# Layer 1 attention of a hybrid decoder trunk: order of VectorE's masks and denominators, place of the routing steps, engine of the softmax divisions

## The reference, cut to what matters

```python
q, k, v = split(rmsnorm(h) @ w_qkv + b_qkv)          # 16 query heads, 2 key heads, 64 wide; then partial rotary
scores = einsum(q_block, [previous_block, this_block] keys) * 64 ** -0.5   # blocks of 128 tokens
m = max(max(where(valid, scores, -inf)), sink);  p = exp(scores - m)
denom = sum(p) + exp(sink - m)
o = (p @ v) / denom
h = h + o @ w_o + b_o
u = rmsnorm(h)                                       # router: best of 4 groups, then the 2 best of its 8 experts
h = h + mixture_of_experts(u)                        # exact dispatch: each token's place in its expert's block is needed
```

## Time and profile before

| what | value |
|---|---|
| median of 3 executions | 2166.18 us (2165.95 to 2168.13) |
| profiled execution, its own time | 2168.93 us |
| span of the profiled execution | 2167.2 us |
| mean granted TensorE clock | 0.976 of full |
| busy: TensorE, VectorE, ScalarE, GpSimd | 2057.6, 1618.5, 1369.8, 240.6 us |

### The profile page before, as it was taken

One profiled execution on the slowest core, in us unless ns is written; L12 is line 12 of the kernel. 1 busy time (PEld: TensorE's weight loads), 2 busy tenths in 40 slices (PEclk: granted clock), 3 DMA queues, 4 the chain that ended last, 5 costly groups with the idle time before them and its releaser, 6 DMA issues. The chain is left out here.

```text
span 2167.2 us, 29972 instructions
## 1 busy us (share of the span) xinstructions
PE 2057.6 (95%) x10496; PEld 1671.1 (77%) x10496; DVE 1618.5 (75%) x2034; ACT 1369.8 (63%) x1754; POOL 240.6 (11%) x250
## 2 busy tenths in 40 slices
PE   8999998898999999999999969987899999999998
PEld 6888887777788888888877846665778888888885
DVE  4552245767888888888984367776798888888886
ACT  5333335553787877887861256665377888887884
POOL 1000000001111111121103310000111111111210
PEclk9999999998999999999999969999999999999999
DMA  4113222115999999999981020010599999999996
GB/s 135 39 59 102 62 88 79 59 60 203 344 383 387 391 386 382 380 377 380 387 288 60 1 88 11 11 59 27 197 351 382 380 385 382 388 388 382 386 372 251
DMA packets 123490, 513.26 MB, mean 237 GB/s; under 512 B 27374, under 2 KB 28491, under 8 KB 89611
## 3 DMA queue, kind: packets, MB, share of 16 engines
q1 hardware_dynamic: 103674, 474.11, 58.2%
q0 software_dynamic: 18576, 33.86, 4.1%
q10 hardware_dynamic: 1152, 4.19, 0.5%
HBM read 495.05 MB, written 50.86 MB: 252 GB/s over the span
## 5 line engine op out<-in xcount | busy, mean ns | idle before, releaser
L526 DVE TENSOR_TENSOR exp_w_lo<-ring_raw,first_w_hi 128x2048 fp32r<-128x2048 f32 x192 | 439.1, 2288 | 34.3 <-ACT first_w_hi L453 34.0
L526 DVE TENSOR_TENSOR exp_w_lo<-ring_raw,exp_w_hi 128x2048 fp32r<-128x2048 f32 x192 | 439.0, 2288 | 28.9 <-ACT exp_w_hi L453 28.8
L453 ACT ACTIVATE exp_w_hi<-ring_raw 128x2048 fp32r<-128x2048 f32 x192 | 367.8, 1918 | 61.6 <-PE exp_up_out L378 30.2
L453 ACT ACTIVATE first_w_hi<-ring_raw 128x2048 fp32r<-128x2048 f32 x188 | 360.8, 1919 | 61.4 <-PE exp_up_out L378 27.9
L378 PE MATMUL exp_gate_out<-exp_w_lo,exp_x_hi 128*128 128x512 f32 x512 | 201.0, 393 | 0.0
L378 PE MATMUL exp_y_out<-exp_w_lo,exp_hid_hi 128*128 128x512 f32 x512 | 200.2, 391 | 0.0
L378 PE MATMUL exp_up_out<-exp_w_lo,exp_x_hi 128*128 128x512 f32 x512 | 199.2, 389 | 0.0
L323 POOL DMA_INDIRECT y_rows<-exp_y,base_rows_y x63 | 77.3, 1228 | 954.2 <-ACT exp_y L473 954.2
L378 PE MATMUL exp_gate_out<-first_w_hi,exp_x_hi 128*128 128x512 f32 x272 | 109.7, 403 | 3.1 <-issue 2.0
L530 DVE TENSOR_TENSOR exp_x_lo<-exp_x_turned,exp_x_hi 128x1024 fp32r<-128x1024 f32 x62 | 75.9, 1225 | 48.7 <-ACT exp_x_hi L457 48.7
L378 PEld LDWEIGHTS exp_up_out<-exp_w_lo,exp_x_hi 128*128 128x128 f32 x512 | 96.1, 188 | 19.9
(11 more groups left out here) (523 smaller groups left out, 4684.0 us busy)
## 6 DMA issues: line engine op xcount, KB each, us to landing
ring_raw<-in_expert_w_gate_dram SPq DMA_DIRECT2D x128, 1024.0 KB, 11.2
ring_raw<-in_expert_w_up_dram SPq DMA_DIRECT2D x128, 1024.0 KB, 11.3
ring_raw<-in_expert_w_down_dram SPq DMA_DIRECT2D x128, 1024.0 KB, 11.1
l0w_raw<-in_ab_w_in_dram SPq DMA_DIRECT2D x48, 256.0 KB, 2.8
finish_y<-y_rows SPq DMA_DIRECT2D x8, 1024.0 KB, 12.1
ring_raw<-in_swa_w_qkv_dram SPq DMA_DIRECT2D x5, 1024.0 KB, 10.2
ring_raw<-y_rows SPq DMA_DIRECT2D x10, 512.0 KB, 5.0
base_h<-in_x_dram ACTq DMA_DIRECT2D x8, 512.0 KB, 6.9
```

What stands on the lines that cost most here:

```text
L453: nc.scalar.activation(split[split_slot(unit)][0][:], raw[raw_slot(unit)][:], ACT.Copy).then_inc(hi_ready, 1)
L526: nc.vector.tensor_tensor(lo[:], raw[raw_slot(unit)][:], hi[:].bitcast(F32), ALU.subtract).then_inc(lo_ready[split_slot(unit)], 1)
```

## The change

`choose_experts` is cut into `choose_first` (group and best expert) and `choose_second`. VectorE's order per G becomes `mask(G+2)`, `out_low(G)`, `denominators(G+1)`. `denominators` no longer divides; ScalarE divides for all four heads in `normalise`, and does it after the exponentials of G + 2 instead of before `out_high(G)`. The routing is spread: half of the choice at g = 3, the other half at g = 0 of the next tile, rows at g = 1, residual, logits and marking at g = 2. `h_root` is cut into `h_squares` (g = 0) and `h_root` (g = 1). The projection's units are dealt 3, 1, 3, 1, 1, 1, 4, 2, and tile 0 gets idle transposes. The end of the stage has another order on TensorE and VectorE.

The diff, cut (`take_top` holds the four operations per expert that stood in the loop of `choose_experts`; `choose_experts` now calls both halves):

```diff
             def turn(G):
                 n = G // GROUPS
-                pe.wait_ge(s["even_normed"], G + 1)
-                pe.wait_ge(s["odd_normed"], G + 1)
+                pe.wait_ge(s["normed"], G + 1)
                 if G == 0:
                     pe.wait_ge(s["q_copied"], 1)
                 else:
                 for k in range(n):
                     nc.tensor.transpose(product[:, BANK + (k % 4) * P:BANK + (k % 4 + 1) * P], c["ident"][:], c["ident"][:])
+            units = {(0, 0): (0, 3), (0, 1): (3, 4), (1, 0): (4, 7), (1, 1): (7, 8), (2, 0): (8, 9), (2, 1): (9, 10), (3, 0): (10, 14), (3, 1): (14, 16)}
+
             def between(n, g, late):
                 u, w = n - 1, n - 2
-                step = 2 * g + late
-                if w >= 0 and step in (0, 2):
-                    turn_rows(w, step // 2)
-                if w >= 0 and step == 4:
+                if w >= 0 and (g, late) == (0, 0):
+                    turn_rows(w, 0)
+                if w >= 0 and (g, late) == (2, 0):
                     route_product(w)
                     if w >= 1:
                         rank(w - 1)
                     if w >= 2:
                         enter(w - 2)
                 if u >= 0:
-                    at = 2 * (step % 4)
-                    project_out(u, step // 4, at, at + 2)
+                    first, end = units[g, late]
+                    project_out(u, first // 8, first % 8, (end - 1) % 8 + 1)
+                elif g >= 1:
+                    if (g, late) == (1, 0):
+                        pe.wait_ge(s["taken"], 2 * T)
+                    idle_turns(6 if late else 12)
+                if w >= 0 and (g, late) == (1, 0):
+                    turn_rows(w, 1)
             def after_attention():
                 a, b = T - 2, T - 1
                 turn_rows(a, 0)
+                project_out(b, 0, 0, 6)
+                turn_rows(a, 1)
                 rank(a - 1)
                 enter(a - 2)
-                project_out(b, 0, 0, 6)
-                turn_rows(a, 1)
                 project_out(b, 0, 6, 8)
                 route_product(a)
                 project_out(b, 1, 0, 4)
                 turn_rows(b, 0)
+                project_out(b, 1, 4, 6)
                 enter(a - 1)
-                project_out(b, 1, 4, 8)
+                project_out(b, 1, 6, 8)
+                turn_rows(b, 1)
                 rank(a)
                 route_product(b, range(4))
-                turn_rows(b, 1)
                 route_product(b, range(4, 8))
                 enter(a)
                 idle_turns(24)
...
-            def norm_even(G):
+            def normalise(G):
                 j, first = G % 3, 0 if G >= GROUPS else P
                 act.wait_ge(s["inv_made"], G + 1)
-                for i in range(2):
+                for i in range(PER):
                     span = slice(i * 2 * P + first, (i + 1) * 2 * P)
                     last = a.activation(masked[j][:, span], masked[j][:, span], ACT.Copy, scale=inv[j][:, i:i + 1])
-                last.then_inc(s["even_normed"], 1)
+                last.then_inc(s["normed"], 1)
...
-            def h_root(u):
+            def h_squares(u):
                 act.wait_ge(s["h_made"], 2 * u + 2)
                 a.activation(r_rows[u] if u + 1 < T else work[0][:], h[:, u], ACT.Square, accum_out=c["sums"][:, u:u + 1])
                 act.drain()
+
+            def h_root(u):
                 a.activation(root[:, u:u + 1], c["sums"][:, u:u + 1], ACT.Sqrt, bias=c["eps"][:], scale=1.0 / 1024).then_inc(s["h_rooted"], 1)
...
             exponents(0)
-            norm_even(0)
+            normalise(0)
             exponents(1)
             for G in range(LAST):
                 g, w = G % GROUPS, G // GROUPS - 2
                 if w >= 0 and g < 2:
                     router_cols(w, g)
                 copy_turned(G)
-                if G + 1 < LAST:
-                    norm_even(G + 1)
+                if w >= 0 and g == 1:
+                    h_root(w)
+                if G == 0:
+                    normalise(1)
                 out_high(G)
                 if G + 2 < LAST:
                     exponents(G + 2)
-                if w >= 0 and g == 1:
-                    h_root(w)
+                if 0 < G < LAST - 1:
+                    normalise(G + 1)
+                if w >= 0 and g == 0:
+                    h_squares(w)
                 for k in W_O_AT.get(G, ()):
                     w_o_high(k)
             for u in (T - 2, T - 1):
                 router_cols(u, 0)
+                h_squares(u)
                 h_root(u)
                 router_cols(u, 1)
...
                 dve.wait_ge(s["prob_made"], G + 1)
                 v.tensor_tensor(inv[j][:], total[j][:], sink_part[j][:], ALU.add)
                 dve.drain()
                 v.reciprocal(inv[j][:], inv[j][:]).then_inc(s["inv_made"], 1)
-                dve.drain()
-                for i in range(2, PER):
-                    span = slice(i * 2 * P + first, (i + 1) * 2 * P)
-                    last = v.tensor_scalar(masked[j][:, span], masked[j][:, span], inv[j][:, i:i + 1], None, ALU.mult)
-                last.then_inc(s["odd_normed"], 1)
...
                 dve.drain()
-                choose_experts(v, dve, c, R, logits, u).then_inc(s["chosen"], 1)
+
+            def choose_one(t):
+                choose_first(v, dve, c, R, logits, t)
+
+            def choose_two(t):
+                choose_second(v, dve, c, R, t).then_inc(s["chosen"], 1)
...
             for G in range(LAST):
                 n, g = G // GROUPS, G % GROUPS
                 u, w = n - 1, n - 2
-                if G + 1 < LAST:
+                if G == 0 or G == LAST - 2:
                     denominators(G + 1)
-                if g == 0 and w >= 0:
-                    residual(w, 1)
                 if 0 < G < LAST - 2:
                     mask(G + 2)
-                out_low(G)
+                if G < LAST - 1:
+                    out_low(G)
                 if G == 0:
                     take_qkv(T - 1)
                     mask(2)
+                elif G < LAST - 2:
+                    denominators(G + 1)
                 if G == 3:
                     store_keys(T - 1, k_turn[1])
-                if g == 2:
-                    if w >= 0:
-                        h_scale(w)
-                    if u >= 0:
-                        residual(u, 0)
+                if g == 0 and w >= 0:
+                    residual(w, 1)
+                    if w >= 1:
+                        choose_two(w - 1)
+                if g == 1 and w >= 0:
+                    h_scale(w)
+                    normed_rows(w)
+                if g == 2 and u >= 0:
+                    residual(u, 0)
                     if w >= 0:
                         take_logits(w, w - 1, w - 2)
+                    if 1 <= w < T - 3:
+                        mark(w - 1)
                 if g == 3 and w >= 0:
-                    normed_rows(w)
-                    if w >= 1:
-                        mark(w - 1)
+                    choose_one(w)
                 for k in W_O_AT.get(G, ()):
                     w_o_low(k)
             a, b = T - 2, T - 1
+            choose_two(a - 1)
             residual(a, 1)
+            out_low(LAST - 1)
+            mark(a - 2)
+            h_scale(a)
+            normed_rows(a)
             dve.wait_ge(s["entered"], a - 1)
             ranks_of(a - 1)
             entries_of(a - 2)
             mark(a - 1)
-            h_scale(a)
-            normed_rows(a)
             residual(b, 0)
             take_logits(a, -1, -1)
+            choose_one(a)
+            choose_two(a)
             gain_last_rows()
             residual(b, 1)
             dve.wait_ge(s["ranked"], a + 1)
             mark(a)
             h_scale(b)
             take_logits(b, -1, -1)
+            choose_one(b)
+            choose_two(b)
             norm_last_rows()
             ranks_of(b)
             mark(b)
```

More of the change, by code:

```diff
@@ L111, in scratch, with take_top, choose_first @@
         self.below, self.slot, self.place = y[:, 354:356], y[:, 356:358], y[:, 358:360]
-def choose_experts(v, dve, c, R, logits, t):
+def take_top(v, dve, c, R, t, k):
     far = c["far"][:, 0:N_EXPERTS]
+    v.tensor_reduce(R.top[:, k, t:t + 1], R.masked, AX.X, ALU.max)
+    dve.drain()
+    v.scalar_tensor_tensor(R.flags, R.masked, R.top[:, k, t:t + 1], far, ALU.is_ge, ALU.mult)
+    dve.drain()
+    v.tensor_reduce(R.idx, R.flags, AX.X, ALU.min)
+    dve.drain()
+    v.tensor_scalar(R.hot[:, t % 2, k], far, R.idx, None, ALU.is_equal)
+    dve.drain()
+def choose_first(v, dve, c, R, logits, t):
     v.tensor_reduce(R.g_top, logits[:, t, 0:4], AX.X, ALU.max)
@@ L126, in choose_experts, with choose_second @@
     v.tensor_tensor(R.masked, R.masked, logits[:, t, 4:36], ALU.add)
-    for k in range(2):
-        dve.drain()
-        v.tensor_reduce(R.top[:, k, t:t + 1], R.masked, AX.X, ALU.max)
-        dve.drain()
```

(22 more changed lines are left out.)

## The result

| | before | changed |
|---|---|---|
| median, runs taken side by side | 2167.31 us (2165.35 to 2169.78, 7 runs) | 2173.61 us (2172.09 to 2177.98, 7 runs) |
| profiled execution: time, span | 2168.93, 2167.2 us | 2173.61, 2171.9 us |
| mean granted clock | 0.976 | 0.982 |

The changed kernel takes 1.0030 of the time before (95% interval 1.0021 to 1.0040): slower by 6.3 us. The forecast was no change (2167.0, range 2159.5 to 2174.0). By the prediction's own measure, which takes over 4.3 us for a change, the outcome is "slower", to which it had given 0.26; the time lies 0.4 us inside the upper edge of its range.

What follows compares the result with a forecast made beforehand. A serial VectorE-ScalarE chain was taken to bound the kernel, 6.28 us per plain group. Stretches of +5.9, +1.1 and -6.1 gave +0.9 on 2168.93, 2169.8; less 2.8 to the median, 2167 us, range 2159.5 to 2174.

Steps and rivals of the forecast that it cites:

- The ring: Serial taking, exponentials, four divisions, turn, copy, weigh: 7.8 us a plain group, where it was 6.28; bounds 7.6 and 8.0.
- the 0.3 for marking: VectorE's extras in the group with residual, logits and marking, 3.8 us against 3.5 of room: 0.3 us late per tile.
- The steady tile: A full four-group tile: four plain groups of 7.8 us plus 2.1 of extras, 33.3 us against 34.2.
- rival 2: TensorE's clock drops in tiles broken by idle pieces: at 0.80 a tile takes 35.6 us, about 2181 in all; chance 0.10.
- Tiles 2 to 7: Stretch from group 7's weigh end to group 31's: 195.2 us before, 196.3 after, +1.1.
- Tiles 0 and 1: Early stretch up to group 7's weigh end, where output weights are split: +5.9 us.
- The idle transposes add little: In the early stretch, the added transposes cost little, as the clock there is low anyway (0.51).
- another 0.7: In the early stretch, the projection unit ahead of group 5's turn waits for weight chunk 6: 0.7 us more.
- The end: After the last group, six projection units go first and fill TensorE's stalls: -6.1 us, bounds -4 and -7.
- The forecast for the stage: Whole attention stage: early stretch +5.9, later tiles +1.1, end -6.1, in total +0.9 us.
- the first (TensorE's pace, 2146): TensorE's work sets the pace, with a shorter ring: tiles of 30 us, about 2146 in all; chance 0.09.
- the third (2166): The change does not matter: mask order and divisions trade off and the end is hidden, 2166 us; chance 0.05.

Runs made afterwards that it cites:

- e11: Changed kernel with one head's division back on VectorE and three on ScalarE: 2167.07 us, ratio 0.9991.
- e2: Changed kernel with two heads' divisions back on VectorE, order and routing as changed: 2157.97 us, ratio 0.9956.
- e12: Changed kernel, all four divisions on ScalarE, with the projection units dealt two to a place everywhere: 2171.94 us, ratio 1.0020.
- e6: Changed kernel with one projection unit moved from ahead of group 3's turn to ahead of group 2's turn: 2171.08 us, ratio 1.0017.
- e5: Kernel before with only the changed order of the end, on TensorE and VectorE: 2163.94 us, ratio 0.9985.
- e8: Changed kernel with the routing undealt: whole choice in group 2, rows and marking in group 3: 2187.05 us, ratio 1.0089.
- e7: Changed kernel with only tile 1's projection units dealt two to a place: 2173.88 us, ratio 1.0032.
- e3: Changed kernel with sum and reciprocal ahead of `out_low` and ScalarE's divisions ahead of `out_high`: 2172.0 us, ratio 1.0026.
- e4: Kernel before with only the mask of G + 2 put ahead of the denominators of G + 1: 2178.14 us, ratio 1.0053.
- e9: Changed kernel with two heads' divisions back on VectorE and projection units dealt two to a place: 2154.07 us, ratio 0.9938.

## Why the prediction was nearly right

**The ring** was right: plain groups of 7.79 us against "7.8 us for a plain group", the next 8.20 and 8.00, the turn released by ScalarE's divisions, VectorE idle ahead of `out_low`. e11 and e2 show it by dose: one division off ScalarE takes 6.5 us from the whole, two take 15.6, and 0.40 us of division out of a group take 0.40 us from it as long as VectorE is not late. One term was right by luck: the 0.3 for marking came as 0.2, but tiles 1 and 2, which mark nothing, have it too; it is the second unit ahead of `weigh` (e12).

**The steady tile** failed by 0.8 us: "33.3" against 34.1. The step was the argument against rival 2, "none of the new pieces comes to 1.5". The pieces ahead of group 2's turn are 1.81 and 1.59 us in the third and fourth tile and 2.74 in the last, so the statement was false; and the 1.35 of the steady tiles was enough for the turn to run at 1.97 for 1.09. The clock falls in each tile from the fifth on; in the third and fourth, at 33.2, it does not. The rival was right in kind and far too large: the clock in the stretch is 0.95, not 0.80, and e6, which fills the piece, gets the 33.2 back and 2.5 us of the whole. The Trainium skill, "TensorE: Matmul & The Clock Gate", section "A second HAM failure mode: psum-queue depth-cycling", warns of small frequent idles between groups of matmuls; the trace agrees in kind (1.97 against 1.09 us), but a mean over the stretch hides it.

**Tiles 2 to 7** were put at +1.1 and came at +5.4 against the first profile. Of the 4.3 missed, 2.4 are the steady tiles' falls (0.8 in each of three) and 1.8 the last tile, 31.9 us (1486.26 to 1518.17) where I had 30.1; one more fall is in it (its third group took 9.79, its turn 1.97), and the other 0.9 was not traced. Seen from the other side, 2.8 of the 5.4 are the first profile's own: before, taken again, needs 198.0 for the same groups, and so does e5. I had measured the rhythm of one execution of before and taken it for that of the kernel.

**Tiles 0 and 1** were put at +5.9 and came at +8.4. But the same code in e8's execution came at +6.2, with W(5) 3.0 later where the prediction had 2.9. So the sum held there, and 2.2 us go with this execution's lower clock (0.84 for 0.92); e7's profile begins in the same slow way, so it is not rare. They begin in group 1, where both executions had waited 2.80 us for the mask; the twelve idle transposes behind that wait took 2.82 us in the changed kernel's profile and 1.53 in e8's, and the turn behind them, late by 1.8 us, made W(1) 2.2 us later:

```profile
1253.43 2.82 PE L2663 MATMUL l_wide<-base_ident 128*128 128x128 f32 x12
```

```profile
1256.76 1.53 PE L2663 MATMUL l_wide<-base_ident 128*128 128x128 f32 x12
```

By W(5) 1.1 of it was left. The rest came behind W(5), with `weigh` of group 6 at 1.97 (1.08 in e8). "The idle transposes add little" is thus right at the high clock only. The wait for chunk 6, priced at "another 0.7", is not the miss: e8 has it too (4.99 us, with the low clock behind it) and keeps the forecast.

**The end** was right: -6.1 against -5.8. e5 shows that the reordering by itself gives 2.4 to 3.0 of it. The forecast for the stage, +0.9, against +8.0 in the first two profiles and 6.3 us in the medians, is short by falls of the clock, in tiles 0 and 1 of this execution and in group 2 of the later tiles, and by the untraced 0.9. That the range's upper edge (2174) held it is partly luck: of the seven executions of the changed kernel five lie below 2174 and two above it.

**What was worse than the forecast is how I reasoned about parts.** Both kernels that were to show that divisions or masks can be taken out of the order (e3, e4) missed, by over 20 us each, for one reason: I followed the chain that I wanted to cut and did not ask which other ring the move closed. In the prediction itself that question had been asked, and its answer held.

**The table loads** cost what the trace of before had: the square root starts 1.29 us after its load (1398.46 to 1399.75). The figure of the Trainium skill, "ScalarE: Activation LUTs", section "What ACT_TABLE_LOAD costs", would have given 2183 us; the trace disagrees again. Of the other rivals, the first (TensorE's pace, 2146) fell with the four divisions in the ring, and e9 shows how near one comes without them; the third (2166) fell with the waits, which all changed place.

## What to carry to other kernels

When an operation is moved out of one engine's critical order, write down the new cycle through all engines, queue order included, and sum it: the sum here was right to 0.01 us for a plain group. Work goes to the engine that is less busy only if it also leaves the ring; with the same deal of units, splitting it over both engines (e9) beat giving all of it to ScalarE (e12) by 17.9 us, and all of it on VectorE was not run. And compare stretches of two executions of the kernel before ahead of crediting a difference of 3 us to a change.

## What the runs showed of the hardware

**The same idle piece does not always cost the same.** In the changed kernel this turn had waited longer than the one at 1405.50 and still ran at full speed:

```profile
1339.09 1.09 PE L2576 MATMUL l_turned<-base_ident,l_work 128*128 128x128 f32 x8 [1.81 <-ACT l_work L2790]
```

In e7 the turn at the same place of the order did fall:

```profile
1340.55 1.97 PE L2576 MATMUL l_turned<-base_ident,l_work 128*128 128x128 f32 x8 [1.81 <-ACT l_work L2790]
```

The idle time is the same to the hundredth. It is not tile 1's units, in which these kernels differ: e8 has them as in the change and its turn at this place fell too. And in one execution of e8 the same place fell in one tile and not in the next (1.67, part of it at the low clock, and 1.09):

```profile
1448.70 1.67 PE L2576 MATMUL l_turned<-base_ident,l_work 128*128 128x128 f32 x8 [1.36 <-ACT l_work L2790]
...
1485.10 1.09 PE L2576 MATMUL l_turned<-base_ident,l_work 128*128 128x128 f32 x8 [1.36 <-ACT l_work L2790]
```

So neither the idle piece nor the order of TensorE's work around it decides by itself whether the clock falls; what else does was not isolated. What helps here is to shorten the piece: e6, at 0.66 to 0.69, has no fall at this place in the steady tiles, and neither has e12.

**Back-to-back operations of ScalarE overlap** by 0.1 us: four divisions of 0.50 end to end in 1.69, three in 1.29. The exponentials start 0.28 us after a taking of 0.38, which is the overlap that the ring's lower bound assumed.
